# A fifth expert's weights loaded ahead of two expert layers, on one core

## The reference

```
x = layer_norm(ALPHA * x + mixer(x), ln1)
f = hier_moe(x)
x = layer_norm(ALPHA * x + f, ln2)

hier_moe:  64 experts; each token goes to the 2 best of the 8 experts of its best group
expert e:  h = silu(xb @ w1[e]) * (xb @ w3[e]);  y = h @ w2[e]
           w1, w3: 1024 x 256,  w2: 256 x 1024
```

## Time and profile before

| | us |
|---|---|
| median of 3 runs | 2958.68 |
| lowest and highest | 2956.83, 2958.93 |
| the profiled execution | 2959.34 |
| its span, from the first to the last instruction | 2957.5 |

### The profile page before, as it was taken

The page is one execution under the profiler, slowest core; times in us unless marked ns, Lnnn a source line. Parts: engine busy times, 40 slices in busy tenths (PEclk is TensorE's granted clock), DMA queues, the critical chain, the costliest instruction groups (busy, mean ns, idle before and its releaser), DMA issues.

```text
span 2957.5 us, 44948 instructions
## 1 busy us (share of the span) xinstructions
PE 2649.1 (90%) x18090; PEld 2025.6 (68%) x18090; DVE 1049.0 (35%) x2379; ACT 907.9 (31%) x1477; POOL 902.6 (31%) x373
## 2 busy tenths in 40 slices
PE   8999897899999999789989699999878678999996
PEld 8996566899999756679989644444457574444443
DVE  3402424643441152364317333232324623323233
ACT  4431461343443136234433121211113521121112
POOL 6860001588788000147868100000014240000000
PEclk9999996999999999689999799999988988999999
DMA  7553410454554322035545499999952156999995
GB/s 244 160 166 111 128 63 23 132 180 148 182 176 155 127 86 86 29 99 158 164 143 168 171 394 421 421 421 421 421 193 101 43 204 244 421 421 421 421 421 218
DMA packets 271164, 643.95 MB, mean 218 GB/s; under 512 B 16816, under 2 KB 191024, under 8 KB 221616
## 3 DMA queue, kind: packets, MB, share of 16 engines
q1 hardware_dynamic: 267952, 635.66, 57.2%
q10 hardware_dynamic: 2176, 3.15, 0.4%
q0 software_dynamic: 896, 3.15, 0.3%
HBM read 637.72 MB, written 4.19 MB: 217 GB/s over the span
## 4 chain that ended last, share of the span: by engine, by line
PE 76%; DMA 11%; DVE 9%; ACT 2%; issue 1%; SPq 0%; ACTq 0%; POOL 0%; DVEq 0%
PE bank L537 35%; PE bank L501 15%; DMA wring<-in_exp_w 11%; PE bank L997 6%; PE bank L982 5%; PE bank L958 3%; PE bank L1006 3%; PE bank L971 3%; PE bank L791 2%; PE bank L569 2%; PE bank L708 1%; PE bank L511 1%; DVE ARENA L1776 1%; DVE XN_rounded L1425 1%; DVE ARENA_rounded L1576 1%
## 5 line engine op out<-in xcount | busy, mean ns | idle before, releaser
L1826 POOL TENSOR_TENSOR wring_rounded<-wring,wring_rounded 128x1024 fp32r<-128x1024 f32 (+1 forms) x336 | 874.1, 2615 | 438.5 <-ACT wring_rounded L1073 437.8
L537 PE MATMUL bank<-SQ_rounded,wring_rounded 128*128 128x272 f32 (+1 forms) x3456 | 653.7, 289 | 28.4 <-POOL wring_rounded L1826 17.8
L537 PEld LDWEIGHTS bank<-SQ_rounded,wring_rounded 128*128 128x128 f32 x3456 | 545.2, 190 | 30.7 <-POOL wring_rounded L1826 13.8
L1073 ACT ACTIVATE wring_rounded<-wring 128x1024 fp32r<-128x1024 f32 (+1 forms) x336 | 374.5, 1117 | 425.8 <-PE bank L537 420.3
L537 PE MATMUL bank<-XN_rounded,wring_rounded 128*128 128x272 f32 (+1 forms) x1728 | 497.5, 288 | 0.0
L537 PE MATMUL bank<-ARENA_rounded,wring_rounded 128*128 128x272 f32 (+1 forms) x3456 | 446.7, 293 | 56.1 <-DVE ARENA_rounded L1566 27.2
L537 PEld LDWEIGHTS bank<-ARENA_rounded,wring_rounded 128*128 128x128 f32 x3456 | 444.1, 194 | 59.6 <-DVE ARENA_rounded L1566 28.5
L537 PEld LDWEIGHTS bank<-XN_rounded,wring_rounded 128*128 128x128 f32 x1728 | 328.7, 190 | 0.2
L997 PE MATMUL bank<-wring,ARENA 128*32 128x512 f32 x2048 | 248.0, 602 | 41.9 <-DVE ARENA L1776 30.4
L1333 ACT ACTIVATE ARENA<-bank 128x512 f32<-128x512 f32 x128 | 76.5, 597 | 662.0 <-PE bank L997 662.0
L501 PE MATMUL bank<-XN,wring 128*128 128x272 f32 (+2 forms) x1088 | 260.1, 405 | 11.8 <-DVE XN L1402 11.8
(11 more groups left out here) (237 smaller groups left out, 2458.0 us busy)
## 6 DMA issues: line engine op xcount, KB each, us to landing
wring<-in_exp_w SPq DMA_DIRECT2D x256, 1024.0 KB, 18.4
ARENA<-in_exp_w SPq DMA_DIRECT2D x128, 1024.0 KB, 17.0
wring<-in_ffn_w_gate SPq DMA_DIRECT2D x44, 1024.0 KB, 5.5
wring<-in_ffn_w_up SPq DMA_DIRECT2D x44, 1024.0 KB, 8.1
wring<-in_ffn_w_down SPq DMA_DIRECT2D x32, 1408.0 KB, 6.2
wring<-in_w_in SPq DMA_DIRECT2D x16, 2048.0 KB, 7.7
wring<-in_conv_w_in SPq DMA_DIRECT2D x24, 512.0 KB, 5.7
wring<-in_attn_w_in SPq DMA_DIRECT2D x5, 2048.0 KB, 8.1
```

The source lines that it names most:

```text
L537: ins = nc.tensor.matmul(o, rounded(a_[:, k, cols]), rounded(x), start=(start and k == 0 and j == 0), stop=(stop and k == len(tiles) - 1 a ...
L1073: st.done(A(rounded(high), w_, ACT.Copy), wh_ready)
L1826: st.done(nc.gpsimd.tensor_tensor(rounded(low), low, part(high), ALU.subtract), wl_ready)
```

## The change

The two tensors `XN` and `SQ` become the halves of one tensor `XS`, whose first 4096 elements are a fifth place for w1 and w3. `W2B` gets a fifth place. The expert 4 (first of group 1) is loaded into the fifth places, once in each layer: w2 behind the w2 of experts 0 to 3, w1 and w3 after the layer norm's last instruction (`x_tile`). The experts 5, 6, 7 and 8 take the places 0 to 3, and expert b from 9 on the place (b - 1) % 4. Each load waits for the expert that had its place: b - 5 for 5 to 8, b - 4 from 9 on. Group 1 is written out on PE, ACT and DVE, groups 1 and 2 on SP; loops run over the rest.

```diff
-        XN = sb("XN", [P, KD, T], twin=True)
-        SQ = sb("SQ", [P, KD, T], twin=True)
+        XS = sb("XS", [P, 2 * KD * T], twin=True)
+        XN = XS[:, 0:KD * T].rearrange("p (k t) -> p k t", k=KD)
+        SQ = XS[:, KD * T:].rearrange("p (k t) -> p k t", k=KD)
...
-        W2B = a(GROUP, 2048)
+        W2B = a(GROUP + 1, 2048)
+        W13B = [RING_B[u][:, 0:SLOT] for u in range(GROUP)] + [XS[:, 0:SLOT]]
...
+        def weight_slot(i, u):
+
+            if isinstance(i, int) and i < 2:
+                return (u, 1) if i == 0 else ((GROUP, 1) if u == 0 else (u - 1, 2))
+            return ((u - 1) % GROUP, i + (u > 0))
+
         def own_and_more(eng, l, group):
-            with eng.Fori(1, NG0) as i:
+            group(1)
+            with eng.Fori(2, NG0) as i:
                 group(i)
...
 (PE, in down and in group; w1 and w3 likewise with m.w13[s], 32 * loads and W13B[s])
-                    pe.wait_ge(m.w2[u], 16 * (i + 1))
+                    s, loads = weight_slot(i, u)
+                    pe.wait_ge(m.w2[s], 16 * loads)
...
 (DVE, ahead of each experts(l))
+            x_at["experts", 0] = st.sent[x_tile]
...
 (SP)
             def expert_weights(l, i, own):
                 for u in range(GROUP):
                     b = GROUP * i + u
+                    s, loads = weight_slot(i, u)
+                    if s == GROUP:
+                        continue
...
-                    sp.wait_ge(M[l].up, b - GROUP + 1)
-                    load_w13(l, u, e)
-                    sp.wait_ge(M[l].y, b - GROUP + 1)
-                    load_w2(l, u, e)
+                    freed = b - GROUP - (isinstance(i, int) and loads == 2)
+                    sp.wait_ge(M[l].up, freed + 1)
+                    load_w13(l, s, e)
+                    sp.wait_ge(M[l].y, freed + 1)
+                    load_w2(l, s, e)
...
                     for u in range(GROUP):
                         load_w2(l, u, u)
-                    with sp.Fori(1, NG0) as i:
+                    load_w2(l, GROUP, GROUP)
+                    sp.wait_ge(x_tile, x_at["experts", l])
+                    load_w13(l, GROUP, GROUP)
+                    for i in (1, 2):
+                        expert_weights(l, i, own=True)
+                    with sp.Fori(3, NG0) as i:
                         expert_weights(l, i, own=True)
```

More of the change, by code:

```diff
@@ L386, in build_model @@
             M.append(MoeSignals(
-                w13=[sem(f"moe{l}_w13_ready{i}") for i in range(GROUP)],
-                w2=[sem(f"moe{l}_w2_ready{i}") for i in range(GROUP)],
+                w13=[sem(f"moe{l}_w13_ready{i}") for i in range(GROUP + 1)],
+                w2=[sem(f"moe{l}_w2_ready{i}") for i in range(GROUP + 1)],
                 **{k: sem(f"moe{l}_{name}") for k, name in (
@@ L965, in down @@
                     pe.wait_ge(m.ht, b + 1)
-                    pe.wait_ge(m.w2[u], 16 * (i + 1))
+                    s, loads = weight_slot(i, u)
+                    pe.wait_ge(m.w2[s], 16 * loads)
                     atleast(pe, m.ys, b)
-                    w2 = W2B[:, u, :].rearrange("p (k n) -> p k n", k=2)
+                    w2 = W2B[:, s, :].rearrange("p (k n) -> p k n", k=2)
                     for q in range(4):
@@ L987, in group @@
                 def group(i):
-                    peeled = isinstance(i, int)
+                    peeled = isinstance(i, int) and i == 0
                     gather(i)
@@ L991, in group @@
                         b = GROUP * i + u
-                        pe.wait_ge(m.w13[u], 32 * (i + 1))
+                        s, loads = weight_slot(i, u)
+                        pe.wait_ge(m.w13[s], 32 * loads)
                         atleast(pe, m.hs, b)
-                        v = RING_B[u][:, 0:SLOT].rearrange("p (m k n) -> p m k n", m=2, k=KD)
+                        v = W13B[s].rearrange("p (m k n) -> p m k n", m=2, k=KD)
                         for k in range(KD):
@@ L1812, in _ @@
             layer_norm(4, "ln1g", "ln1b", 1)
+            x_at["experts", 1] = st.sent[x_tile]
             experts(1)
@@ L1865, in _, with load_w13, load_w2 @@
             sp.dma_start(H[:, :, :], h0_dram).then_inc(h_loaded, 16)
-            def load_w13(l, u, e):
-                v = RING_B[u][:, 0:SLOT].rearrange("p (m x) -> p m x", m=2)
+            def load_w13(l, s, e):
+                v = W13B[s].rearrange("p (m x) -> p m x", m=2)
                 for j, name in enumerate(("exp_w1_2", "exp_w3_2")):
                     sp.dma_start(v[:, j, :], w[name][l][bass.ds(e, 1)].rearrange("o (p k) n -> p (o k n)", p=P)
[L1871 to L1875, removed]
+                                 ).then_inc(M[l].w13[s], 16)
+            def load_w2(l, s, e):
+                sp.dma_start(W2B[:, s, :], w["exp_w2_2"][l][bass.ds(e, 1)].rearrange("o (p k) n -> p (o k n)", p=P)
+                             ).then_inc(M[l].w2[s], 16)
             def expert_weights(l, i, own):
```

## The result

The changed kernel is slower: 2969.12 us (median of 6) against 2958.8 beside it, a ratio of 1.0039 with a 95% interval of 1.0027 to 1.0051. I had forecast 2953.1. Its profiled execution took 2968.87 us with a span of 2967.0, 9.5 us more than before.

| part of the span, us | before | after | difference |
|---|---|---|---|
| start to the end of group 0, layer 0 | 1720.6 | 1720.0 | -0.6 |
| groups 1 to 15, layer 0 | 436.5 | 434.9 | -1.6 |
| from there to the end of group 0, layer 1 | 329.0 | 334.3 | +5.3 |
| groups 1 to 15, layer 1 | 436.7 | 435.2 | -1.5 |
| from there to the end | 34.7 | 42.6 | +7.9 |

A forecast was written before the change was run, and what follows sets the result against it. PE's pace bounds about ten groups of each layer, DMA the last five; gains of 2.6 + 3.0 = 5.6 us, all else 0, take the median 2958.68 to 2953.1 us, range 2950.7 to 2955.0.

The forecast's parts named there:

- the 12.6 us at most: Last groups of both layers: time lost to DMA, 6.2 and 6.4 us, all that earlier weights can give.
- The fifth expert ahead: Before each layer's first expert: three more transfers, 7.5 us, fit into 25 and 31 us of idle DMA at no cost.
- the gate of expert 11: Its second matrix waits for expert 7's down product; landing in 7.4 and 7.8 us less 4.8 caps the gain at 2.6 and 3.0.
- comes through whole: Behind expert 11's gate: 4.9 and 4.5 of 7.47 us go, the remaining 2.6 and 3.0 us all shorten the layers.
- I had bounded this at 0.8 us and taken 0: Code block fetched among loads behind expert 11's gate: up to 0.8 us off each layer's gain, taken as 0.
- I take 0 in time: Group 1 written out on four engines: same instructions and same step as the loop, so 0 us.
- is not part of that: PE's 2.41 us before the last product at layer 0's end: releaser is "issue", not a transfer, so outside the 12.6 us.
- The rivals: Whole lead arrives 2946.1 us (0.08), stop at loop's entry 2957.9 (0.09), no effect 2958.7 (0.06), slower 3013.3 (0.08).
- the slower one: Jump back in the group loop waits for code, 2.4 us in each of 14 turns: 3013.3 us, chance 0.08.
- the loop's entry: Rival: leaving written group 1 for the loop stops PE 2.4 us, leaving 0.2 and 0.6 us gain: 2957.9 us, chance 0.09.
- the 128 KiB: PE's code space by the skill: jump back is free while the body fits, so the change costs nothing here.

The follow-up runs named there:

- the changed kernel with filler: Changed kernel plus 180 empty instructions at the head of PE's program, shifting the PE code behind them: 2971.03 us.
- that with the slot: Changed kernel with the head of PE's loop placed at slot 144 of a 256 block, by a jump over filler: 2955.21 us, ratio 0.9981.
- the five measurements here: One loop to a count read first: changed kernel 0.9959; kernel before, nothing ahead, 0.9966 and 0.9979; only expert 4's second matrix ahead, 0.9956 and 0.9967.
- the written-out one with the slot: Kernel before with group 1 written out, nothing loaded ahead, head of PE's loop at slot 144: 2960.45 us, ratio 0.9999.

## Why the prediction was wrong

- *What bounds the kernel, and the 12.6 us at most:* right.
- *The fifth expert ahead costs nothing before the first expert:* right; its first matrices landed at 1661.6 + 21.1 = 1682.7 us, before the first up product.
- *The places stop the lead at the gate of expert 11:* right. The load lands in 4.8 us, from an empty queue, in both layers. The landing came 2.9 and 3.3 us earlier after the end of group 0 than before (forecast 2.6 and 3.0). The 0.3 us more are the gate itself: group 1, written out, is that much shorter, and the load is issued 38.6 us after the end of group 0 instead of 38.9.
- *What passes the gate "comes through whole":* half right, and 2.6 and 3.0 us were too large. 1.6 and 1.5 us arrived. I took the lead from when transfers land. By what DMA moved less passes the gate. These are the 32 us from 10 to 42 us after the end of group 0 of layer 0, before and then changed:

```profile
1730.62:1762.62 32.00, 30.16 (x216) 15.15 (x216) 9.02 (x26) 6.50 (x14) 0.00 (x0) 1.00 1.01 417
```

```profile
1729.99:1761.99 32.00, 30.15 (x216) 15.00 (x219) 9.30 (x26) 6.43 (x14) 0.00 (x0) 1.00 0.89 343
```

  74 GB/s less is (74 / 421) x 32 = 5.6 us of DMA's time, where I had 4.9, and 7.47 - 5.6 = 1.9 us are left. In layer 1 it is 416 and 342 GB/s, the same 5.6 us, where I had 4.5. Over the 388 us behind that both kernels move 421 GB/s.

  By the landings the lead is lost a little later. The next second matrix, issued at 1764.3, landed at 1772.3 us, 3.9 us after the transfer before it (1759.8 + 8.6 = 1768.4) instead of 2.5. In that stretch a block of PE's code was fetched. In layer 1 the step from 2542.7 to 2546.8 us, 4.1 us, goes with a block at 2543.9. The view of that load and the queues from 1764 to 1772 us:

```profile
L1887 SPq DMA_DIRECT2D ARENA<-in_exp_w x1: 333/333/333, 1764.3 to 1764.3; - x1
...
DMA to landing us min/median/max: 8.0/8.0/8.0
```

```profile
q8 instruction: 1, 0.02, 0.8%
```

  I had bounded this at 0.8 us and taken 0. No run took the fetch away alone, but in some it came elsewhere. In layer 1 of the changed kernel with filler, and of that with the slot, no block comes between 38 and 88 us, and 38 and 145 us, after the end of group 0. There the landings keep their step and stay 2.8 us ahead of before; with the next block that lead falls to 2.1 and 2.0 us, and the groups gain 2.0. So a block takes 0.7 to 1.6 us of the lead, and even there 1 us of the forecast 3.0 is missing.
- *Group 1 written out, "I take 0 in time":* **the step that failed.** I costed the instructions and their fetch, not what their length does to a jump far behind them. Its cost was 3.6 + 3.2 us at the two exits, 4.7 us of lower clock in the tail, and some of the 1.7 us between the layers, where both kernels change clock but at other moments (not taken apart). With the slot of the loop set, the time is 0.19% below before, though the groups' part of it is 3.6 us and not 5.6.
- *The exit's 2.41 us "is not part of that":* right for DMA, but I left it there. It was the row to ask further, since it was the one wait with a block of code beside it.
- *The rivals:* the slower one had the mechanism (a jump to code that is not held) at the wrong jump. The turns of the loop stay at 28.69 us, and the loop's entry is free. I leaned on the 128 KiB that the Trainium skill gives PE in the same section, and read them as "near code is held"; here a jump forward by 1.6 blocks stalled for 3.5 to 4.1 us in three kernels, so that reading is not what the chip did. It made me give "slower" too low a chance.

## What to carry to other kernels

Before code is added in front of a loop or a jump, look at the taken jumps behind it, and at the longest duration of each, not its median: one that skips more than a block can be cheap by luck of its place. A rarely used copy of a large body that is skipped by a jump is better folded into one loop whose count is read first; in the five measurements here that took 0.2 to 0.4% off the kernel before, with loads ahead or without. And loading further ahead is worth only what passes the next full buffer. The slack of the tightest load (its time from issue to landing less that of an empty queue) gives an upper bound before anything is built: here 2.6 and 3.0 us, of which 1.6 and 1.5 arrived.

## What the runs showed that was not expected

- A jump of PE to code not held takes 3.5 to 4.1 us (six such jumps: 4079, 3727, 3729, 3468, 3834 and 3643 ns), one to held code 0.22 to 0.40. Even with held code, a middle turn of the unused loop takes PE some 0.75 us from start to start, 0.45 of it in its two jumps.
- An empty PE instruction with a semaphore increment takes about 0.16 us (180 in 28.4 us).
- Waits of 2.1 to 2.4 us at the end of layer 1 are no sure sign for the clock: it stayed at full speed in the kernel before and in the written-out one with the slot (tails 34.7 and 34.5 us), and was at half for 3.4 us behind the wait in the changed kernel with filler and with the slot (35.8 and 35.9). In the kernels with waits of 5.2 to 5.6 us it fell during the wait or within 0.2 us of its end, and the tail was 41.7 to 43.1 us long.
